# Sample rows held as four bands of 32 partitions, front-only and loop-only buffers overlaid, ten pairs of places for expert weights instead of nine

## The reference

```python
mod = (silu(c) @ w_ada + b_ada).reshape(B, 6, 1, D)      # w_ada (1024, 6144)
sh1, sc1, g1, sh2, sc2, g2 = ...
h = rms_norm(x, norm1_g) * (1 + sc1) + sh1
proj = h @ w_in                                          # (1024, 1536)
a, new_pool = pool_mix(proj[..., :512], ...)             # trailing means over 2, 4, 8, 16 rows, then a grouped matmul
b, new_conv = conv_mix(proj[..., 512:], ...)             # gated, depthwise conv of width 31, layer norm, silu, matmul
gates = sigmoid(h @ gate_w + gate_b)                     # (1024, 2048)
merged = gates[..., :D] * a + gates[..., D:] * b
x = x + g1 * (merged @ w_out)
h2 = rms_norm(x, norm2_g) * (1 + sc2) + sh2
x = x + g2 * moe(h2)        # router: top 4 of 32 experts; each expert three 1024x1024 matrices, clamped SwiGLU
y = rms_norm(x, final_g)
```

## Time and profile before

| what | value |
|---|---|
| median of the runs | 1153.06 us |
| span of the profiled execution | 1150.3 us (the median is 2.8 us above it) |
| PE busy | 1122.8 us, 98% |
| DVE, ACT, POOL busy | 497.9, 181.4, 29.8 us |
| moved by DMA | 456.15 MB, mean 397 GB/s |
| weight queue q1 | 452.35 MB, 94.9% of the 16 DMA engines' span |
| first loop item starts | 228.88 us |
| last down product ends | 1137.72 us |

### The profile page before, as it was taken

The page is one execution under the profiler, slowest core; times in us unless marked ns, Lnnn a source line. Parts: engine busy times, 40 slices in busy tenths (PEclk is TensorE's granted clock), DMA queues, the critical chain, the costliest instruction groups (busy, mean ns, idle before and its releaser), DMA issues.

```text
span 1150.3 us, 16135 instructions
## 1 busy us (share of the span) xinstructions
PE 1122.8 (98%) x5962; PEld 457.5 (40%) x5963; DVE 497.9 (43%) x1134; ACT 181.4 (16%) x343; POOL 29.8 (3%) x78
## 2 busy tenths in 40 slices
PE   8999999999999999999999999999999999999996
PEld 6676675633333333333333333333333333333332
DVE  3498425653344433444333433343334433333334
ACT  4101301311111111111111111111111111111112
POOL 4002300000000000000000000000000000000000
PEclk9999999999999999999999999999999999999999
DMA  9988688699999999999999999999999999999995
GB/s 342 374 288 297 245 305 303 229 419 417 427 428 428 428 428 428 428 428 428 428 428 428 428 428 428 428 428 428 428 428 428 428 428 428 428 428 429 426 422 228
DMA packets 59022, 456.15 MB, mean 397 GB/s; under 512 B 7237, under 2 KB 26497, under 8 KB 31349
## 3 DMA queue, kind: packets, MB, share of 16 engines
q1 hardware_dynamic: 54880, 452.35, 94.9%
q10 hardware_dynamic: 4117, 3.47, 1.2%
HBM read 454.40 MB, written 1.40 MB: 396 GB/s over the span
## 4 chain that ended last, share of the span: by engine, by line
PE 77%; DMA 21%; DVE 1%; issue 0%; SPq 0%; ACT 0%; DVEq 0%
PE bank L1731 46%; DMA arena<-in_exp_w_up 10%; DMA arena<-in_exp_w_gate 10%; PE bank L1509 6%; PE bank L1456 4%; PE bank L1758 4%; PE bank L1675 4%; PE bank L1596 2%; PE bank L1813 1%; PE bank L1579 1%; PE bank L1683 1%; PE bank L1430 1%; PE bank L1749 1%; PE bank L1687 1%; PE bank L1378 1%; PE bank L1689 0%
## 5 line engine op out<-in xcount | busy, mean ns | idle before, releaser
L1731 PE MATMUL bank<-ring,arena 128*64 128x512 f32 x2112 | 469.9, 595 | 10.2 <-DMA ring<-in_exp_w_gate 9.7
L1731 PEld LDWEIGHTS bank<-ring,arena 128*64 128x64 f32 x2112 | 146.3, 137 | 310.0 <-issue 283.7
L1731 PE MATMUL bank<-arena 128*64 128x512 f32 x1056 | 235.9, 595 | 4.2 <-DMA arena<-in_exp_w_gate 4.0
L1731 PEld LDWEIGHTS bank<-arena 128*64 128x64 f32 x1056 | 73.6, 137 | 153.8 <-issue 138.5
L821 ACT ACTIVATE arena<-arena 32x256 f32<-32x256 f32 x136 | 56.0, 412 | 421.1 <-DVE arena L1200 419.9
L1291 DVE TENSOR_SCALAR arena<-bank 128x512 f32<-128x512 f32 x33 | 22.8, 691 | 166.6 <-PE bank L1731 166.6
L1284 DVE TENSOR_SCALAR arena<-bank 128x512 f32<-128x512 f32 x33 | 22.8, 691 | 166.5 <-PE bank L1731 166.5
L1306 DVE TENSOR_TENSOR arena<-bank,biases 128x512 f32<-128x512 f32 x66 | 42.5, 686 | 109.9 <-PE bank L1731 109.9
L1269 DVE TENSOR_TENSOR x<-x,bank 128x512 f32<-128x512 f32 x132 | 84.5, 681 | 12.6 <-PE bank L1758 12.6
L834 ACT ACTIVATE arena<-arena 128x512 f32<-128x512 f32 x33 | 20.8, 629 | 353.8 <-DVE arena L1284 353.8
L1758 PE MATMUL bank<-arena 64*128 64x512 f32 x264 | 65.6, 615 | 0.0
(11 more groups left out here) (312 smaller groups left out, 739.8 us busy)
## 6 DMA issues: line engine op xcount, KB each, us to landing
ring<-in_exp_w_gate SPq DMA_DIRECT2D x42, 2048.0 KB, 27.8
ring<-in_exp_w_up SPq DMA_DIRECT2D x41, 2048.0 KB, 28.2
ring<-in_exp_w_down SPq DMA_DIRECT2D x40, 2048.0 KB, 29.1
arena<-in_exp_w_gate SPq DMA_DIRECT2D x21, 2048.0 KB, 25.7
arena<-in_exp_w_up SPq DMA_DIRECT2D x20, 2048.0 KB, 27.3
arena<-in_exp_w_down SPq DMA_DIRECT2D x20, 2048.0 KB, 30.0
ring<-in_w_ada SPq DMA_DIRECT2D x24, 1024.0 KB, 10.7
ring<-in_gate_w SPq DMA_DIRECT2D x8, 1024.0 KB, 8.6
```

Source lines behind the costliest of these rows:

```text
L1731: ins = mm(out[64 * hh:64 * hh + 64, :], lhs(k), w[:, D * (k % 2) + HALF * hh:D * (k % 2) + HALF * (hh + 1)], start=(done is y_mm and k == ...
```

## The change

PAIRS becomes 10 and TURN 5 (10 pairs x 3 = 30 = 5 experts; PE goes through the body six times and two experts stay behind it). Four pairs lie in the arena. The buffers that the loop needs are moved into its first 3568 columns (`LOOP_END`); the four regions `PAIR_A` to `PAIR_D` behind it first hold front buffers and then weights. SP loads pair 6 (`PAIR_C`) after `pm_mm`, `act_c_ready` and `cst_mm`; pair 7 (`PAIR_A`) and pair 8 (`PAIR_B`) one ring pair later, after `merged_ready` and `rows_out[1]`; pair 9 (`PAIR_D`) after `logit_mm` and `ssq2`. The sample is loaded straight into `xs`; its sum of squares is added over the bands by a matmul with `same_row` (`sample_sum`), which DVE now makes at the start. ACT's `spread` calls no longer wait for `merged_ready`; the sample's g2 row follows when h2 of the sample is made.

```diff
-ARENA = 17660
-EARLY_PAIR, LATE_PAIR, LAST_PAIR = ARENA - 4096, 7168, 3072
-PAIRS = 9
-TURN = 3
-SPLIT, HALVED, LAST_HALVES = 4, 3, (1, 2, 3, 5)
+PAIRS = 10
+TURN = 5
+LOOP_END = 3568
+PAIR_A, PAIR_B, PAIR_C, PAIR_D = (LOOP_END + 2 * SLOT * i for i in range(4))
+FAR_PAIRS = (PAIR_C, PAIR_A, PAIR_B, PAIR_D)
+ARENA = LOOP_END + 8 * SLOT
+SPLIT, HALVED, LAST_HALVES = 4, 4, (1, 2, 3, 5)
...
-            sp.dma_start(x[0:NS_TOK, 2, :], x_sample[0]).then_inc(x_ld[2], 16)
+            sp.dma_start(xs[:, :], x_sample[0].rearrange("n (q d) -> q n d", q=4)).then_inc(x_ld[2], 16)
...
             for i in order:
                 if i == order[3]:
+                    sp.wait_ge(pm_mm, KD)
                     sp.wait_ge(act_c_ready, 1)
                     sp.wait_ge(cst_mm, 4)
+                    load(1, PER_EXPERT)
+                if i == order[4]:
+                    sp.wait_ge(merged_ready, KD)
+                    load(1, PER_EXPERT + 1)
                     sp.wait_ge(rows_out[1], 64)
-                    load(1, PER_EXPERT)
+                    load(1, PER_EXPERT + 2)
...
             sp.wait_ge(logit_mm, TT)
-            load(1, PER_EXPERT + 1)
-            sp.wait_ge(h2_ready, TT + 1)
-            load(1, PER_EXPERT + 2)
+            sp.wait_ge(ssq2, 6)
+            load(1, PER_EXPERT + 3)
             sp.wait_ge(base_ready, 1)
...
+            spread(sh2b, sh2s, 0, 1, spread_ld[1])
             act.wait_ge(a2rows, 1)
...
-            act.wait_ge(merged_ready, KD)
-            spread(sh2b, 0, 1, spread_ld[1])
             act.wait_ge(rows_out[1], 64)
-            spread(a2b, 1, 0, spread_ld[1])
+            spread(a2b, a2s, 1, 0, spread_ld[1])
...
+            squares = view(PAIR_A + 2 * D, QUAD)
+            dve.wait_ge(x_ld[2], 16)
+            step(v.tensor_tensor(squares, xs, xs, ALU.mult))
+            v.tensor_reduce(part_sum[:, 0:1], squares, AX, ALU.add).then_inc(parts_ready, 1)
             dve.wait_ge(colT, 1)
             v.tensor_copy(c_cols[:, :], bank[5][:, 0:2 * KD]).then_inc(c_cols_ready, 1)
+            dve.wait_ge(parts_mm, 1)
+            v.tensor_scalar(stat[:, 10:11], bank[7][:, 504:505], 1.0 / D, EPS, ALU.mult, ALU.add).then_inc(mean2, 1)
...
-            add_output(NS_TOK, 2, [(slice(256 * q, 256 * (q + 1)), bank[6][32 * q:32 * q + 32, 0:256]) for q in range(4)])
+            add_output(xs, g1s, bank[6][:, 0:QUAD], part[:, 0:QUAD])
...
+            def turn_sample(dst, src):
+                for c in range(2):
+                    ins = tr(dst[:, P * c:P * (c + 1)], src[:, P * c:P * (c + 1)], ident[:, :])
+                return ins
+            def sample_sum(nth):
+                pe.wait_ge(parts_ready if nth == 1 else ssq2, 1)
+                mm(bank[7][:, 504:508], same_row[:, :], part_sum[:, :], start=True, stop=True).then_inc(parts_mm, 1)
...
             pe.wait_ge(x2_ready, 1)
-            turn(2, range(KD), bank[3]).then_inc(x2_turned, 1)
+            sample_sum(2)
+            turn_sample(bank[3][:, 0:QUAD], xs).then_inc(x2_turned, 1)
...
+            pe.wait_ge(sqrt_ready, 2)
             out_part(bank[7][:, :], 1, 0, 2)
```

More of the change, by code:

```diff
@@ L72 @@
 F_END = -(-N_FRONT // RING) * RING
-USES = [len([f for f in range(N_FRONT) if f % RING == s and FRONT[f][0] != "none"]) for s in range(RING)]
+USES = [len([f for f in range(N_FRONT) if f % RING == s and FRONT[f][0] != "none"]) for s in range(RING)] + [0]
 CONV_SPLIT = 18
@@ L161, in build @@
[L161 to L169, removed]
+        xgT, gsig, gmin, actT = (view(HALF * i, HALF) for i in range(4))
@@ new lines, in build @@
+        hS = view(PAIR_A, KD, TOK)
+        xns = view(PAIR_A + 2560, QUAD)
+        up_ext = view(PAIR_B + 512, CT, PEXT)
+        act_c = view(PAIR_B + 512, CT, TOK)
+        rows = view(PAIR_B + 1784, 3, HALF)
+        wsum = view(PAIR_B + 3320, 2, PEXT)
+        cols = view(PAIR_B + 3956, N_COLS)
+        c_cols = view(PAIR_B + 4000, 2 * KD)
+        csig = view(PAIR_B + 4016, 16)
+        scc = view(PAIR_B + 4032, 2 * KD)
+        cst_rows = view(PAIR_B + 4048, E)[0:2, :]
+        shc = view(PAIR_B + 4080, 2 * KD)
@@ new lines, in build @@
+        sig_g = view(PAIR_D, CT, TOK)
+        ln_mean, ln_var = view(PAIR_D, CW), view(PAIR_D + CW, CW)
+        shT = view(PAIR_D + 1152, KD, 32)
+        group_of = view(PAIR_D + 1408, TOK)
+        x2T = merged[:, :, 0:P]
+        bada = view(PAIR_D + 2304, HALF)[0:4, :]
+        g1b = view(PAIR_D + 2304, D)
+        n2rows = view(PAIR_D + 3328, HALF)[0:64, :]
+        part = view(PAIR_D + 3328, HALF)
+        g1s = view(PAIR_D + 3840, QUAD)
+        ada_bias = [view(2560, HALF), rows[:, 0, :]]
@@ L781, in _, with root @@
             a.activation(stat[:, 31:32], stat[:, 30:31], ACT.Sqrt)
-            def root(t, count):
-                a.activation(stat[0:ROWS[t], 4 + t:5 + t], stat[0:ROWS[t], t:t + 1], ACT.Sqrt, scale=1.0 / D,
-                             bias=stat[0:ROWS[t], 11:12]).then_inc(sqrt_ready, 1)
+            def root(t, total):
+                a.activation(stat[:, 4 + t:5 + t], total, ACT.Sqrt, scale=1.0 / D, bias=stat[:, 11:12]).then_inc(sqrt_ready, 1)
             act.wait_ge(x2_ready, 1)
-            a.activation(h2[0:NS_TOK, 2, :], x[0:NS_TOK, 2, :], ACT.Square, accum_out=stat[0:NS_TOK, 2:3]).then_inc(ssq2, 1)
-            act.wait_ge(ssq2, 1)
-            root(2, 1)
+            a.activation(g1s, xs, ACT.Square, accum_out=part_sum[:, 0:1]).then_inc(ssq2, 1)
+            act.wait_ge(parts_mm, 2)
+            root(2, bank[7][:, 504:505])
             for hh in range(2):
@@ L825, in _ @@
             move_squares()
-            act.wait_ge(h2_ready, TT + 1)
-            for q in range(4):
-                ins = a.activation(quadrant(xs, q), quarter(x[0:NS_TOK, 2, :], q), ACT.Copy)
-            ins.then_inc(xs_ready, 1)
             act.wait_ge(base_ready, 1)
@@ L1068, in _, with add_output @@
             wo_reads = [0]
-            def add_output(r, t, cuts, after=0):
+            def add_output(row, gain, src, to, after=0):
                 if after:
                     dve.wait_ge(x2_ready, after)
-                parts = [view(12288 + cs.start, cs.stop - cs.start)[0:r, :] for cs, _ in cuts]
-                for part, (cs, src) in zip(parts, cuts):
-                    v.tensor_tensor(part, src, g1b[0:r, t // 2, cs], ALU.mult).then_inc(wo_ev, 1)
-                wo_reads[0] += len(cuts)
+                v.tensor_tensor(to, src, gain, ALU.mult).then_inc(wo_ev, 1)
+                wo_reads[0] += 1
@@ new lines, in add_prompt, with norm2_prompt, norm2_sample @@
+            def add_prompt(t, cs, src, after):
+                add_output(x[:, t, cs], g1b[:, cs], src, part[:, cs.start % HALF:cs.start % HALF + cs.stop - cs.start], after)
+            def norm2_prompt(t):
+                step(v.scalar_tensor_tensor(out=h2[:, t, :], in0=x[:, t, :], scalar=stat[:, 4 + t:5 + t], in1=a2b,
+                                            op0=ALU.mult, op1=ALU.mult))
+                v.tensor_tensor(h2[:, t, :], h2[:, t, :], sh2b, ALU.add).then_inc(h2_ready, 1)
+            def norm2_sample():
+                step(v.scalar_tensor_tensor(out=part[:, 0:QUAD], in0=xs, scalar=stat[:, 6:7], in1=a2s, op0=ALU.mult, op1=ALU.mult))
+                for q in range(4):
+                    ins = v.tensor_tensor(quarter(h2s, q), part[strip(q), 0:QUAD], sh2s[strip(q), :], ALU.add)
+                ins.then_inc(h2_ready, 1)
@@ L1407, in _ @@
             pe.wait_ge(xn_ready, TT)
+            turn_sample(bank[6][:, QUAD:2 * QUAD], xns).then_inc(xT, 1)
             for k in range(4):
```

324 lines of the change are left out of this document (149 added, 175 removed).

## The result

The changed kernel takes 1164.35 us (median of 6 runs, 1156.42 to 1167.12), before 1153.01 in the same runs: ratio 1.0088, 95% interval 1.0068 to 1.0107 (this ratio is taken over the runs; the two medians alone give 1.0098). So it is slower by about 0.9%. The forecast was 1147.9, range 1146.0 to 1151.0. The profiled execution spans 1163.5 us, 13.2 more than before.

The account below looks back on a forecast made before the run. DMA was taken to bound the kernel: from its last idle moment, near 262 us, the remaining bytes at 428 GB/s set the end. 1150.3 - 4.9 (tenth pair) - 0.3 (routing) = 1145.1, plus 2.8 to the median: 1147.9 us, range 1146.0 to 1151.0.

Parts of the forecast that it names:

- The rows fetched among bulk transfers: Routing: a2 rows issued at about 168 us land by 182 even at 13.4 us; DVE asks at 194; cost 0.
- `sqrt_ready` 2: PE's new wait before the bank 7 product at 200.7 us; ACT's root comes at about 193, so it is hidden.
- Tenth pair, -4.9: Expert loop: one more pair filled at DMA's last hole, so later pairs land 4.9 us earlier; bounds 0 and 4.9.
- Pauses: PE's pauses in the expert loop: 14.9 of 19.8 us left, the first, near 2 us, before the large expert.
- HALVED, TURN, lead kept, 0: Expert loop: one more halved refill, fewer ways through the body, and DMA's rate kept during the large expert: each 0.
- Pairs 7 and 8 at about 182: Weight loads before the loop: both pairs follow pair 2 at about 182 us, into a stretch where DMA was empty.
- Turning and routing, -0.3: Routing stretch on PE: two turnings of 128 rows and one matmul replace eight of 32; 0.3 us won, bounds 0 and 0.5.
- Start, 0, bounds -0.5 and 1.0: Kernel start: shorter DVE sample work gains nothing, as PE waits for `w_in`; between 0.5 us won and 1.0 lost.
- Rival A: Longer loop body outgrows PE's instruction store, stalls at each way back: 1150.0 to 1200 us, 1182.5 at the median; chance 0.13.
- Rival B: Tenth place buys nothing, through idle DMA in the large expert's second item or slower DMA: 1152.8 us; chance 0.07.
- The 2.8 us between span and median: Added to the forecast span of 1145.1 us, since the runs' median stands 2.8 us above the profiled span.

Follow-up runs that it names:

- run 4: Changed kernel with the sample's bands and the sample itself each loaded by four transfers, and the sh2 fetch behind the a2 write: 1148.13 us, 0.9948.
- run 1: Changed kernel with the sample's g1, sh2 and a2 bands each fetched by four transfers of 32 rows, same bytes and order: 1149.55 us, 0.9971.
- run 5: run 4 with nine pairs and the old PAIRS, TURN, HALVED and order of halves, no pair 9: 1153.4 us, 0.9999.
- run 6: run 4 with twelve filling matmuls instead of three ahead of PE's sum over the bands at the start: 1148.37 us, 0.9952.
- run 2: Changed kernel with the fetch of sh2 moved behind the write of the a2 rows, transfer shapes unchanged: 1157.17 us, 1.0033.
- run 8: run 4 with one more fetch of g1's bands ahead of the a2 write, as four transfers of 32 rows: 1149.06 us, 0.9966.
- run 7: run 4 with one more fetch of g1's bands ahead of the a2 write, as one 4 x 32 x 1 KB transfer: 1149.31 us, 0.9975.
- run 11: run 4 with only the sh2 broadcast (128 rows of 4 KB) moved back ahead of the a2 write: 1149.44 us, 0.9973.
- run 10: run 4 with two more fetches of g1's bands, each 4 x 32 x 1 KB, ahead of the a2 write: 1159.64 us, 1.0056.
- run 3: Changed kernel with SP holding back pair 6 until the write of the a2 rows has landed: 1160.48 us, 1.0055.
- run 9: Changed kernel with only the sh2 bands cut into four transfers of 32 rows, order unchanged: 1155.03 us, 1.0025.

## Why the prediction was wrong

The step that failed is **"The rows fetched among bulk transfers"**, which ends in 0. It let the fetch of the a2 rows be issued at about 168 us, as if the write ahead of it landed as before, and put 13.4 us on the fetch alone. The write, which now had two fetches more ahead of it on its queue, got no price at all. It landed 33.2 us after its last issue instead of 5.2, and the fetch was issued at 201.65. The 13.4 would not have bounded it either: those rows are of transfers with rows of 4 KB, and the two transfers of 4 x 32 x 1 KB have a shape that the trace of before doesn't contain. Shape was weighed at the start ("shorter rows") and not here.

Its price came through a second step, the one on `sqrt_ready` 2: "ACT's transfer issues end near 175 instead of 190.5". They ended at 205.86, and at 178.5 even in run 4. That sentence named what is exposed if the cover goes ("PE would wait with all routing behind it"), but gave it no price and no chance. It was the rival that the list lacked: from a landing of about 187 us on (run 1, PE waits 0.5) each further microsecond is about one of PE (191.5: 4.1; 196.4: 10.0; 201.65: 14.6).

The other steps:
- *Tenth pair, -4.9*: right. 4.8 in the trace, 5.0 between run 5 and 6. Pauses 15.0 (14.9), 2.1 before the large expert ("near 2").
- *HALVED, TURN, lead kept, 0*: right; nothing beside the pair is left in run 5.
- *Pairs 7 and 8 at about 182*: half right. Pair 7 went at 183.68, pair 8 at 201.64, because it waits for the write; in run 4 both went by 184. The tenth pair kept its worth.
- *Turning and routing, -0.3*: right where nothing waits. From ACT's last gate sigmoid to the first item run 4 takes 70.1 us, before 70.3.
- *Start, 0, bounds -0.5 and 1.0*: too narrow. The gate products end 1.3 us later in the changed kernel (159.85 against 158.57), 1.1 in run 4, and 0.2 earlier in run 6. Over the twelve traces of kernels with the change it is from -0.2 to 4.6 (run 2), 1.4 in the middle; single executions differ by more than the term.
- *Rival A* is out: no q8 packet falls between 358 and 1090 us, and the items stay 26.93 apart across the five ways back. The first time through the body, q8 fetched six blocks of 16 KB between 248 and 358 us. Of the two figures of the Trainium skill ("Runtime: NRT & Kernel Launch", "Instruction fetch mechanics") the larger one, 128 KiB for PE, agrees with this trace, the window of two blocks does not.
- *Rival B* is out (run 5).

That the forecast of 1147.9 is only 0.2 below run 4 is in part luck. Its span of 1145.1 is 1.5 below run 4's 1146.6, mostly by the start (1.1). The 2.8 us between span and median made that good: they were read from one execution of the kernel before, and in run 4 the same distance is 1.5, in the changed kernel 0.9.

## What to carry to other kernels

When a small transfer is moved ahead of a synchronous write on the same queue, ask for its shape as well as its bytes: the outermost dimension of a pattern with a band index in front (4 x 32 x 256) is 4, and next to full-rate bulk traffic its 128 rows of 1 KB then take over 20 us. What counts is how many packets stand on the fullest engine when the bulk transfers fill it: each took about 0.65 us here. Four transfers of 32 rows cost nothing that could be seen ahead of that moment (run 8), and part of the 19.1 us of run 1 behind it. Issue a write that others wait for first, and price the whole list of work behind an in-order engine's wait, not only the transfer. Order alone left 1157.17 us here, strips alone 1149.55, and both, with the sample's load by four transfers, 1148.13. The intervals of the last two overlap, so the time doesn't show what order adds to strips; the landing does (19.1 against 7.2 us).

## What the runs showed of the hardware

- The write landed 5 to 11 us after its last issue in the kernel before and in runs 2, 4, 7, 8 and 11, and 27 to 33 us after it behind two transfers of 4 x 32 x 1 KB (run 10, changed kernel), with q1 at 98% of the engines' time in the changed kernel. Runs 3, 1 and 9 lie between (17.4, 19.1, 25.9).
- Two queues that both have work on an engine pass packet for packet, whatever the size: 142 packets of q1 (nearly all data packets of 16 KB) and 141 of q10 between 176 and 182 us in run 4. Behind q1's 16 KB packets a 1 KB packet so costs its own queue about 0.65 us on that engine (190.39 to 191.09 and on, changed kernel).
- A transfer of the pattern 4 x 32 x 256 holds up its own queue on four engines only: in run 10 96 of 128 packets issued behind it passed by 180.5 us and the other 32 from 195.2 on.
- Issues slow down when such transfers are queued: the write's four issues took 4.8 to 5.3 us with two of them ahead (changed kernel, runs 3 and 10) and 1.1 to 1.7 with one or none. Two issues in run 2 took 9.52.
- PE's granted clock fell to 0.79 at 195 to 200 us and to 0.50 at 200 to 210 after PE had stopped at 193.3; the next sixteen matmuls took 1.25 us more.
